# A hybrid encoder block on one core: its opening reordered on all engines

## The chip, the cores and the metric

The kernel runs on one core of a Trainium2 chip. The metric is the device time of one execution in microseconds (us). The engines are TensorE (PE in the profile, PEld for its weight loads), VectorE (DVE), ScalarE (ACT), GpSimd (POOL) and SyncE (SP, which issues DMAs). The granted TensorE clock has two levels, 1.2 and 2.4 GHz; 1.00 in a row is the upper one and 0.50 the lower.

## The reference

One block over 512 tokens of width 1024, in float32. x is RMS-normalised to h, h is projected by w_in, three branches run on the projections, and their gated outputs are merged, projected and added to x.

```
h = rms_norm(x, norm_g); proj = h @ w_in
A: mLSTM scan over q_a, k_a (after a causal conv), v_a, input and forget gates if_a
B: scores = sum_h relu(rot(qi_h) . rot(ki) / 8) * wi_h   # 8 index heads of 64
   per query the best 128 admissible keys, then attention of 8 heads on them
M: mem_h = rms_norm(mem, mem_norm_g); kv = mem_h @ w_mem_kv    # 256 memory tokens
   attention of 4 heads of 256 on the memory
x + (sum_j sigmoid(gate_j) * (y_j @ w_branch_j)) @ w_out
```

Rotary embeddings need the cosine and sine of position times inv_freq (angles).

## The kernel before

A float32 operand is split in two float32r parts: the high part is a rounding copy on ScalarE, the low part is the operand minus the high part, on VectorE. A product of two operands is three TensorE products: high by high, high by low, low by high.

**Panels.** The weights come in panels of up to 512 columns. A panel has two halves (kh = 0, 1) of four k tiles of 128 rows. For each half: SP loads it in w_raw (L324), ScalarE makes w_hi (`split_hi`, L751, 128x2048), VectorE makes w_lo (`split_lo`, L1069), and TensorE runs one block for each output tile: 12 products of 512 columns (4 k tiles by 3, `products`, L391). The buffer has one place for each half, so w_hi of the next panel waits until TensorE has used this one's half. A panel's blocks are numbered as slots through both halves (0 to 3 with two tiles). A hook is other TensorE work put ahead of the block of a slot; it waits for its inputs with the whole TensorE queue behind it.

**Order.** Each engine executes its own list in the order in which it is written; the engines meet at semaphores only. No planner is at work. The opening goes as follows.

1. x tiles 1, 2, 3, 0 (`FIRST_TILES`): ScalarE sums squares (L768), VectorE makes the variance, GpSimd the power -1/2 (L1570), VectorE scales the rows by it and by norm_g (L1092). TensorE turns each tile in two halves of four 128x128 transposes (L442), ScalarE writes the high parts hT_hi (L774) and VectorE the low parts hT_lo (L1100). mem's two tiles go the same way into memT_hi and memT_lo, but GpSimd scales them, in two passes each (L1581, L1582).
2. Index panel 1 (`IDX1`): the index queries of tokens 128 to 511 (three tiles), with the transposes of the later x tiles as hooks.
3. The angles: VectorE waits for inv_freq and positions (L1123 to L1134, twelve steps on 128x256 values), ScalarE takes the sines (L796, L797), VectorE copies them into tables for the index heads (L1141), GpSimd multiplies them with gains for branch B (L1590, eight products).
4. Index panel 2 (`IDX2`, the narrow panel): index key, head weights and mLSTM gates, 80 columns, with a panel turn of its own; its rows arrive by four DMAs (L348, L350).
5. Four memory panels 0 to 3 (`KV`) make the keys and values of the memory. Their hooks carry the index branch: `ki_transposes`, `gates_to_rows`, `idx_transposes` in panel 0, then eight `logit`s in each of panels 1 to 3, two a slot. A logit has six (or three) products on 64 rows; ScalarE applies relu (L829), VectorE adds it to the scores (L1220, L1222). logit(u) waits for the relu of logit u - 3. ScalarE's Exp and Ln for the mLSTM gates (L839, L840, a table load each) stand in panel 1 before the relus. The prefix scans over the gates (`gate_scans`, L1206 to L1211) stand on VectorE at the end of panel 1. The mean squares of the memory keys are a 128x2048 square on GpSimd (L1595) and a sum on VectorE (L1252) in panel 2.
6. The first cross-attention panel (`MS`) has `gates_to_columns` (L534) ahead of its first block, which waits for the gate scans (`gate_rows`) and for all 24 score sums, and `km_transposes` (L544) ahead of its fourth.

After that come the branches M, B and A and the merging, untouched by the change.

Of the kernel before, what the change touches and what calls it, by code (L numbers as in the profile page):

```python
# [23 lines left out]
FIRST_TILES = (1, 2, 3, 0)  # L24
A_HEADS, A_HD = 4, 256
# [61 lines left out]
IDX2 = _plan.take(1, 0, (1, 0, 0, 0))  # L87
# [37 lines left out]
def hybrid_block(nc, x, mem, positions, norm_g, mem_norm_g, w_in, conv_w, conv_b, mlstm_gate_b,  # L125
                 mlstm_norm_g, dsa_q_norm_g, dsa_k_norm_g, mem_q_norm_g, mem_k_norm_g,
                 w_mem_kv, w_branch, w_out, inv_freq, out):
    ctx = ExitStack()
    with ctx:
# [38 lines left out]
        idx2_raw = arena[:, 8 * D - 2 * KH * I_COLS:8 * D].rearrange("p (h k n) -> p h k n", h=2, k=KH)  # L168
        vec_rows = arena[0:92, 5 * D:5 * D + P]
        gain_rows = arena[:, 7 * D + P:7 * D + 3 * P]  # L170
        memT_hi = y_hi
        memT_lo = y_lo

        kiT = [y[:, 0:2, MEM:] for y in (y_hi, y_lo)]
        qiT = [[y[:, 2 * t:2 * t + 2, MEM:] for t in range(1, TT)] for y in (y_hi, y_lo)]
# [3 lines left out]
        ki_rot = yF[:, 3584:4096].rearrange("p (t n) -> p t n", t=TT)  # L181
# [9 lines left out]
        qi_b = arena[:, 8 * D:8 * D + 512]  # L191
        kiF = arena[0:I_COLS, 8 * D + 512:9 * D]

        km_raw = merged[:, 2048:4096]
        km_sq = arena[:, 4096:6144]
# [57 lines left out]
        w_hi_done, w_lo_done, w_used = sem("w_hi_done"), sem("w_lo_done"), sem("w_used")  # L253
        proj_done = [sem(f"proj_done{b}") for b in range(4)]
# [11 lines left out]
        idx_turned, idx_copied, ki_copied = sem("idx_turned"), sem("idx_copied"), sem("ki_copied")  # L266
        ki_turned, ki_rotated, q_split = sem("ki_turned"), sem("ki_rotated"), sem("q_split")
# [47 lines left out]
        def _(sp):  # L315
            def load(p, parts):

                for kh in range(2):

                    narrow = isinstance(p, int) and p == IDX2[0] + 1  # L320
                    sp.wait_ge(w_lo_done, IDX2[0] * 2 + (kh - 1) if narrow else p * 2 + (kh - 1))
                    at = 0
                    for w, c0, n in parts:
                        sp.dma_start(w_raw[:, kh, :, at:at + n], w_cols(w, kh * KH, c0, n)).then_inc(w_landed[kh], 16)  # L324
                        at += n
# [7 lines left out]
            sp.dma_start(w_raw[:, 0], w_cols(wi, 0, C_QI, 512)).then_inc(w_landed[0], 16)  # L333
            load_x(FIRST_TILES[2:])
            sp.dma_start(w_raw[:, 1], w_cols(wi, KH, C_QI, 512)).then_inc(w_landed[1], 16)
# [11 lines left out]
            for kh in range(2):  # L347
                sp.dma_start(idx2_raw[:, kh, :, 0:I_HD + I_HEADS], w_cols(wi, kh * KH, C_KI, I_HD + I_HEADS))\  # L348
                    .then_inc(idx2_landed, 16)
                sp.dma_start(idx2_raw[:, kh, :, I_HD + I_HEADS:], w_cols(wi, kh * KH, C_IF, 2 * A_HEADS))\  # L350
                    .then_inc(idx2_landed, 16)
# [32 lines left out]
        def _(pe):  # L384
            mm, turn = nc.tensor.matmul, nc.tensor.transpose

            def products(ps, lhs, rhs, k0, first, last):

                for k in range(KH):
                    for j, (a, b) in enumerate(((0, 0), (0, 1), (1, 0))):  # L390
# [43 lines left out]
            def x_transposes(i):  # L434

                pe.wait_ge(x_scaled, i + 1)
                for half in range(2):
                    n = 2 * i + half
                    if n >= 4:
                        pe.wait_ge(xT_lo, n - 3)  # L440
                    for k in range(4):
                        ins = turn(att[n % 4][:, k * P:(k + 1) * P],  # L442
                                   x_sc[:, i % 2, (half * 4 + k) * P:(half * 4 + k + 1) * P], ident[:, :])
                    ins.then_inc(x_turned, 1)
# [5 lines left out]

            pe.wait_ge(consts, 4)
            for i in range(2):
                x_transposes(i)

            panel(IDX1[0], [(t, 0, tokens(hT, t), w_as_rhs(512), 512, [(xT_lo, 2 * FIRST_TILES.index(t) + 2), None])
                            for t in range(1, TT)],
                  {1: [lambda: x_transposes(TT - 2)], 2: [lambda: x_transposes(TT - 1)], 4: [lambda: x_transposes(TT)],
                   5: [lambda: x_transposes(TT + 1), vector_transposes]})  # L460

            pe.wait_ge(xT_lo, 2 * TT)
            for kh in range(2):
                pe.wait_ge(w_lo_done, IDX2[0] * 2 + kh + 1)
                ins = products(banks[0][0:I_COLS, :], [lambda k, k0, w=w: w[:, kh, k, 0:I_COLS] for w in (w_hi, w_lo)],
                               all_tokens(hT)(kh), kh * KH, kh == 0, kh == 1)
                ins.then_inc(proj_done[0] if kh else w_used, 1)
# [10 lines left out]
            def gates_to_rows():  # L478
                pe.wait_ge(gates_copied, 1)
                pe.wait_ge(vec_copied, 1)  # L480
                pe.wait_ge(xT_lo, 2 * (TT + MT))
                for kind in range(2):
                    for t in range(TT):
                        ins = turn(att[kind][0:A_HEADS, t * P:(t + 1) * P],
# [3 lines left out]
            def idx_transposes():  # L488
                pe.wait_ge(qi_rotated, 3)
                pe.wait_ge(ki_rotated, 1)  # L490
                pe.wait_ge(gates_read, 1)
                for t in range(3):
                    for j in range(4):
                        ins = turn(att[t][:, j * P:(j + 1) * P], qi_rot[:, t, j * P:(j + 1) * P], ident[:, :])
# [1155 lines left out]
```

## Time and profile before

| | |
|---|---|
| device time, median of 3 runs | 1050.3 us (1049.99 to 1051.4) |
| span of the profiled execution (its own time: the page gives none beside the span) | 1049.9 us |
| TensorE busy | 1022.1 us, 97% |
| VectorE busy | 563.3 us, 54% |
| ScalarE busy | 403.7 us, 38% |
| GpSimd busy | 85.5 us, 8% |
| mean granted clock | 0.993 |

The span runs from the first to the last instruction of one execution. Busy time is the time with an instruction of that engine at work; a matmul's end is modelled, so consecutive ones overlap in the record. The time of a block is best read from the chain of waits, where a piece lasts until the next one begins.

### The profile page before, as it was taken

How to read it: one execution, taken by the hardware profiler on the slowest of the kernel's cores; microseconds unless marked ns; L12 is line 12 of the kernel's file. 1: busy time of each engine (PE TensorE's matmuls, PEld its weight loads, DVE VectorE, ACT ScalarE, POOL GpSimd, SP SyncE). 2: the span in 40 equal slices, each digit the busy share in tenths (PEclk: the TensorE clock that was granted, in tenths of full speed). 3: DMA queues.
4: the chain of work that ended last, by engine and by line, in shares of the span. 5: the costliest groups of instructions: out<-in, count | busy, mean ns of one | idle time of the engine just before them, and what ended most of it. 6: DMA issues, size and time to landing. Idle time of an engine off the chain costs nothing.

```text
span 1049.9 us, 13242 instructions
## 1 busy us (share of the span) xinstructions
PE 1022.1 (97%) x4965; PEld 856.2 (82%) x4965; DVE 563.3 (54%) x919; ACT 403.7 (38%) x567; POOL 85.5 (8%) x66
## 2 busy tenths in 40 slices
PE   5799999999999999999999999999999999999998
PEld 4577787778888888898898798787987888788887
DVE  4968686666854544544545645327353243532352
ACT  5264453433534434434435453444334422412230
POOL 1501010110110110110110000000000000000000
PEclk9899999999999999999999999999999999999999
DMA  9144421222233223223232222231312424234331
GB/s 300 41 138 132 126 86 41 70 62 61 61 91 90 75 75 90 75 75 90 73 98 81 66 95 61 61 120 53 107 61 61 120 81 120 81 86 144 130 101 60
DMA packets 110664, 95.42 MB, mean 91 GB/s; under 512 B 6344, under 2 KB 100900, under 8 KB 110628
## 3 DMA queue, kind: packets, MB, share of 16 engines
q1 hardware_dynamic: 109812, 94.37, 29.9%
q10 hardware_dynamic: 816, 0.56, 0.2%
q8 instruction: 24, 0.39, 0.2%
q14 instruction: 12, 0.10, 0.0%
HBM read 92.82 MB, written 2.10 MB: 90 GB/s over the span
## 4 chain that ended last, share of the span: by engine, by line
PE 91%; DVE 6%; ACT 2%; issue 1%; DMA 0%; POOL 0%; DVEq 0%; ACTq 0%; POOLq 0%
PE proj L391 78%; PE att L686 2%; PE att L618 2%; PE att L673 2%; PE att L633 2%; PE att L582 1%; DVE w_lo L1069 1%; PE att L562 1%; ACT w_hi L751 1%; PE att L625 1%; PE att L512 1%; PE att L608 1%; DMA yF<-x_in 0%; DVE score L1266 0%; DVE small L1264 0%
## 5 line engine op out<-in xcount | busy, mean ns | idle before, releaser
L1069 DVE TENSOR_TENSOR w_lo<-w_raw,w_hi 128x2048 fp32r<-128x2048 f32 (+2 forms) x94 | 198.4, 2111 | 271.7 <-ACT w_hi L751 269.9
L391 PE MATMUL proj<-hT_hi,w_hi 128*128 128x512 f32 (+1 forms) x648 | 257.2, 397 | 0.0
L391 PE MATMUL proj<-hT_hi,w_lo 128*128 128x512 f32 (+1 forms) x648 | 253.0, 390 | 0.0
L391 PE MATMUL proj<-hT_lo,w_hi 128*128 128x512 f32 (+1 forms) x648 | 252.7, 390 | 0.0
L751 ACT ACTIVATE w_hi<-w_raw 128x2048 fp32r<-128x2048 f32 (+2 forms) x94 | 159.3, 1695 | 211.4 <-PE proj L391 211.2
L391 PEld LDWEIGHTS proj<-hT_hi,w_hi 128*128 128x128 f32 (+1 forms) x648 | 121.6, 188 | 28.6 <-issue 4.0
L391 PEld LDWEIGHTS proj<-hT_hi,w_lo 128*128 128x128 f32 (+1 forms) x648 | 121.4, 187 | 25.9
L391 PEld LDWEIGHTS proj<-hT_lo,w_hi 128*128 128x128 f32 (+1 forms) x648 | 121.5, 188 | 25.7 <-issue 1.1
L391 PE MATMUL proj<-w_hi,hT_hi 128*128 128x384 f32 (+2 forms) x408 | 138.6, 340 | 2.8 <-DVE w_lo L1069 2.8
L391 PE MATMUL proj<-w_hi,hT_lo 128*128 128x384 f32 (+2 forms) x408 | 133.4, 327 | 0.0
L391 PE MATMUL proj<-w_lo,hT_hi 128*128 128x384 f32 (+2 forms) x408 | 133.4, 327 | 0.0
L391 PEld LDWEIGHTS proj<-w_hi,hT_hi 128*128 128x128 f32 x408 | 78.4, 192 | 6.8 <-DVE w_lo L1069 3.2
L391 PEld LDWEIGHTS proj<-w_lo,hT_hi 128*128 128x128 f32 x408 | 78.5, 192 | 3.5 <-issue 1.9
L391 PEld LDWEIGHTS proj<-w_hi,hT_lo 128*128 128x128 f32 x408 | 78.3, 192 | 1.4
L391 PE MATMUL proj<-y_hi,w_hi 128*128 128x512 f32 x192 | 76.0, 396 | 2.1 <-DVE y_lo L1075 1.2
L391 PE MATMUL proj<-y_hi,w_lo 128*128 128x512 f32 x192 | 74.9, 390 | 0.0
L391 PE MATMUL proj<-y_lo,w_hi 128*128 128x512 f32 x192 | 74.9, 390 | 0.0
L391 PE MATMUL proj<-w_hi,y_hi 128*128 128x512 f32 x128 | 52.3, 408 | 1.6 <-DVE w_lo L1069 1.6
L391 PE MATMUL proj<-w_lo,y_hi 128*128 128x512 f32 x128 | 50.7, 396 | 0.0
L391 PE MATMUL proj<-w_hi,y_lo 128*128 128x512 f32 x128 | 50.7, 396 | 0.0
L391 PEld LDWEIGHTS proj<-y_hi,w_hi 128*128 128x128 f32 x192 | 36.1, 188 | 10.0 <-issue 2.9
L391 PEld LDWEIGHTS proj<-y_hi,w_lo 128*128 128x128 f32 x192 | 36.1, 188 | 7.6
(229 smaller groups left out, 1153.0 us busy)
## 6 DMA issues: line engine op xcount, KB each, us to landing
w_raw<-w_in_in SPq DMA_DIRECT2D x72, 512.0 KB, 4.0
w_raw<-w_in_in SPq DMA_DIRECT2D x80, 256.0 KB, 3.2
w_raw<-w_mem_kv_in SPq DMA_DIRECT2D x8, 1024.0 KB, 5.1
w_raw<-w_branch_in SPq DMA_DIRECT2D x16, 512.0 KB, 5.0
yF<-x_in SPq DMA_DIRECT2D x8, 512.0 KB, 7.3
w_raw<-w_branch_in SPq DMA_DIRECT2D x16, 256.0 KB, 3.5
w_raw<-w_out_in SPq DMA_DIRECT2D x4, 1024.0 KB, 5.0
w_raw<-w_in_in SPq DMA_DIRECT2D x2, 1024.0 KB, 11.2
```

What stands on the lines that cost most here:

```text
L391: ins = mm(ps, lhs[a](k, k0), rhs[b](k, k0), start=(first and k == 0 and j == 0), stop=(last and k == KH - 1 and j == 2))
L512: ins = mm(att[u % 4][:, half * MEM:half * MEM + w], q[a], kiT[b][lo:lo + I_HD, half, 0:w], start=(j == 0), stop=(j == 2))
L562: ins = mm(att[1 + t // 2][:, (t % 2) * MEM:(t % 2 + 1) * MEM], m_qT[:, e, t * P:(t + 1) * P], kh_[:, bass.ds(h * 512 + e * MEM, MEM)], st ...
L582: ins = mm(att[1 + e][:, :], m_vh[:, m, e * P:(e + 1) * P], m_pT[:, m, :], start=(m == 0), stop=(m == MT - 1))
L608: ins = turn(att[c][:, t * P:(t + 1) * P], b_rc[:, (2 * t + c) * P:(2 * t + c + 1) * P], ident[:, :])
L618: mm(att[(t + 2) % 4][:, 0:(t + 1) * P], b_qT[:, t * P:(t + 1) * P], b_kT[:, 0:(t + 1) * P], start=True, stop=True).then_inc(b_scores, 1)
L625: ins = turn(att[(t + 2) % 4][:, s * P:(s + 1) * P], score[:, off(t) + s * P:off(t) + (s + 1) * P], ident[:, :])
L633: ins = mm(att[2][:, s * P:S], b_raw[:, s, 2 * P:3 * P], b_pT[:, s, s * P:S], start=(s == 0), stop=(s == TT - 1))
L673: ins = mm(att[bank][:, c:c + n], a_kT[:, e, s * P:(s + 1) * P], a_qT[:, e, s * P:S], start=(e == 0), stop=(e == 1))
L686: ins = mm(att[t][:, 0:A_HD + 1], a_at[:, c:c + P], a_v[:, s, :], start=(s == 0), stop=(s == t))
L751: A_(w_hi[:, kh, :, 0:n], raw[:, kh, :, 0:n], ACT.Copy).then_inc(w_hi_done, 1)
L1069: V.tensor_tensor(w_lo[:, kh, :, 0:n], raw[:, kh, :, 0:n], w_hi[:, kh, :, 0:n].bitcast(F32), ALU.subtract).then_inc(w_lo_done, 1)
```

## The change

The opening is put in another order on every engine, and some of its work changes its form:

- ScalarE no longer loads norm_g; it issues positions (as a contiguous array of 4 columns) and inv_freq first. SP issues: x tiles 1 and 2, norm_g, both halves of the first weights, x tiles 3 and 0, the narrow panel's rows in one DMA, mem, the small ones.
- VectorE starts with the angles up to the reduction by multiples of 2 pi, before the first variance; the last four steps follow after the fourth low part of x.
- The first half of the first weights is split for each k tile (four high and four low parts of 128x512), and TensorE's first block waits for each.
- x tiles are turned by halves in the order `TURNS`; block order is 1/0, 2/0, 1/1, 2/1, 3/0, 3/1 (tile/half).
- mem rows are scaled on VectorE in one pass.
- The narrow panel has buffers of its own and is no panel turn any more; the memory panels move up by one.
- Query and key of the index branch are split in high and low parts before they are transposed; 64 rows of high and 64 of low parts stand under each other. A logit is two products on 128 rows over the whole width. This takes 24 + 8 transposes instead of 12 + 4, and eight copies on ScalarE (`idx_copy`); low parts by VectorE are `q_lows` and `k_lows`.
- The logits are spread by `LOGIT_SLOTS`: none in slot 0 of panel 1, then 2, 2, 2; 3, 2, 3, 2 in panel 2; 3, 2, 2, 1 in panel 3.
- Squares of the memory keys come from ScalarE, two of 256 columns with each of the four evacuations. GpSimd's table products wait for the sixteenth score sum.
- Exp and Ln move from panel 1 to panel 2, the gate scans from panel 1 to the end of panel 3.

```diff
+TURNS = ((0, 0), (1, 0), (0, 1), (1, 1), (2, 0), (2, 1), (3, 0), (3, 1), (4, 0), (4, 1), (5, 0), (5, 1))
+LOGIT_SLOTS = ((), (0, 0, 2, 4, 6), (6, 9, 11, 14, 16), (16, 19, 21, 23, 24))
-IDX2 = _plan.take(1, 0, (1, 0, 0, 0))
+IDX2 = _plan.take(0, 0, (1, 0, 0, 0))
 # SP
             load_x(FIRST_TILES[:2])
+            sp.dma_start(g_row, norm_g.partition_broadcast(P)).then_inc(g_landed, 16)
+            for kh in range(2):
+                sp.dma_start(w_raw[:, kh], w_cols(wi, kh * KH, C_QI, 512)).then_inc(w_landed[kh], 16)
             load_x(FIRST_TILES[2:])
+            sp.dma_start(idx2_raw, w_idx2).then_inc(idx2_landed, 16)
 # TensorE
+            for n in range(4):
+                x_transposes(n)
+            idx_block(1, 0, 1, [(w_first_lo, 1), (w_first_lo, 2), (w_first_lo, 3), (w_lo_done, 1)])
+            idx_block(2, 0, 2)
+            pe.wait_ge(w_lo_done, 2)
+            idx_block(1, 1, 3).then_inc(proj_done[1], 1)
+            x_transposes(4)
+            x_transposes(5)
+            idx_block(2, 1, 4).then_inc(proj_done[2], 1)
+            x_transposes(6)
+            x_transposes(7)
+            idx_block(3, 0, 5).then_inc(w_used, 1)
+            idx_block(3, 1, 6).then_inc(proj_done[3], 1)
+            x_transposes(8)
+            x_transposes(9)
...
+            def q_transposes(f):
+                bank = (0, 1, 2, 0, 2, 0)[f]
+                t = f // 2
+                pe.wait_ge(q_low, t + 1)
+                if f == 0:
+                    pe.wait_ge(vec_copied, 1)
+                    pe.wait_ge(xT_lo, 2 * (TT + MT))
...
+                q = idxT[2 * (t - 1) + h // 4][:, h % 4 * P:(h % 4 + 1) * P]
+                n = (t + 1) * P
+                mm(att[u % 4][:, 0:n], q, idxT[6][:, 0:n], start=True, stop=False)
+                mm(att[u % 4][:, 0:n], q, idxT[7][:, 0:n], start=False, stop=True).then_inc(logits, 1)
 # hooks of memory panel i
+                    return {1: [ki_transposes, lambda: q_transposes(0), lambda: q_transposes(1)],
+                            2: [lambda: q_transposes(2), lambda: q_transposes(3)], 3: [gates_to_rows]}
+                marks = LOGIT_SLOTS[i]
+                hooks = {s: [lambda u=u: logit(u) for u in range(marks[s], marks[s + 1])] for s in range(4)}
+                if i == 1:
+                    hooks[0] = [lambda: q_transposes(4), lambda: q_transposes(5), k_transposes]
 # ScalarE
             square(0)
             square(1)
+            act.wait_ge(w_landed[0], 16)
+            for k in range(KH):
+                A_(w_hi[:, 0, k, :], w_raw[:, 0, k, :], ACT.Copy).then_inc(w_first_hi if k < KH - 1 else w_hi_done, 1)
+                if k < 2:
+                    x_high(k)
             x_high(2)
+            split_hi(0, 1, 1, 512)
             x_high(3)
             square(2)
             square(3)
...
+            x_high(8)
+            x_high(9)
+            split_hi(1, 0, KV[1] + 1, 512)
+            x_high(10)
+            split_hi(1, 1, KV[1] + 1, 512, (3, 1))
+            x_high(11)
             act.wait_ge(proj_done[0], IDX2[2][0] + 1)
             A_(kiF, banks[0][0:I_COLS, :], ACT.Copy).then_inc(bank_empty[0], 1)
+            for t in range(3):
+                q_highs(t)
 # ScalarE, memory panel i
-                if i == 1:
+                if i == 2:
                     act.wait_ge(gate_abs, 1)
                     steps.then(A_(rows[:, 3], rows[:, 2], ACT.Exp, scale=-1.0))
                     A_(rows[:, 3], rows[:, 3], ACT.Ln, bias=1.0).then_inc(gate_ln, 1)
...
+                        for e in range(2):
+                            g = m * M_HEADS + 2 * i + e
+                            A_(km_junk, banks[b][:, e * M_HD:(e + 1) * M_HD], ACT.Square, accum_out=kss[:, g:g + 1])\
+                                .then_inc(km_squared, 1)
+                            act.wait_ge(km_squared, i * 4 + m * 2 + e + 1)
 # VectorE
+            rotate_queries(1)
+            x_low(8)
+            x_low(9)
+            split_lo(1, 0, 512)
+            rotate_queries(2)
+            x_low(10)
+            split_lo(1, 1, 512)
+            x_low(11)
...
+            rotate_queries(3)
+            for t in range(3):
+                q_lows(t)
...
-                if i == 1:
+                if i == 2:
+                    dve.wait_ge(km_squared, 8)
+                    V.tensor_scalar(kss, kss, 1.0 / M_HD, EPS, ALU.mult, ALU.add).then_inc(km_var, 1)
+                if i == 3:
                     gate_scans()
-                if i == 2:
-                    dve.wait_ge(km_squared, 1)
-                    then(V.tensor_reduce(kss, km_sq.rearrange("p (g n) -> p g n", n=M_HD), AX, ALU.add))
 # GpSimd
             pool.wait_ge(small_landed, 16 * 4)
+            pool.wait_ge(summed, 16)
```

## Rows read from the trace of the kernel before

**Rows 1.** The page: busy time of the engines, and engines' shares of the chain.
```profile
PE 1022.1 (97%) x4965; PEld 856.2 (82%) x4965; DVE 563.3 (54%) x919; ACT 403.7 (38%) x567; POOL 85.5 (8%) x66
...
PE 91%; DVE 6%; ACT 2%; issue 1%; DMA 0%; POOL 0%; DVEq 0%; ACTq 0%; POOLq 0%
```

**Rows 2.** Waits of TensorE: us in total, times, longest us.
```profile
PE att L442 <- DVE arena L1092: 9.4, 1, 9.4
PE proj L391 <- DVE w_lo L1069: 4.5, 2, 2.8
PE att L442 <- DVE hT_lo L1100: 3.4, 1, 3.4
PE att L512 <- DVE w_lo L1069: 2.2, 1, 2.2
PE att L449 <- DVE y_lo L1100: 1.8, 1, 1.8
...
PE att L442 <- POOL arena L1582: 0.9, 1, 0.9
```

**Rows 3.** The chain of waits in order of time: start us, us, what.
```profile
16.19 5.49 PE proj L391 x12
...
33.02 0.43 DVE arena L1130
...
33.94 2.01 DVE arena L1130
...
44.26 7.94 PE proj L391 x24
...
66.32 1.31 PE att L494 x12
...
96.75 4.53 PE proj L391 x12
...
105.42 1.25 PE att L512 x12
106.67 2.94 PE proj L391 x12
...
122.80 8.41 PE proj L391 x36
```

**Rows 4.** One stretch: us, busy of PE, PEld, DVE, ACT, POOL, PEclk, DMA, GB/s.
```profile
40.00:50.00 10.00, 8.07 (x25) 6.26 (x26) 8.45 (x18) 3.17 (x7) 5.54 (x8) 0.54 0.01 2
```

**Rows 5.** Timeline of ScalarE: start us, us, line, operation [idle before].
```profile
71.37 1.91 ACT L751 ACTIVATE w_hi<-w_raw 128x2048 fp32r<-128x2048 f32 x1
73.29 1.28 ACT L839 ACT_TABLE_LOAD   x1
74.58 0.63 ACT L839 ACTIVATE merged<-merged 4x512 f32<-4x512 f32 x1
```

**Rows 6.** Timeline of VectorE, five rows between 8 and 92 us.
```profile
8.02 1.28 DVE L1092 SCALAR_TENSOR_TENSOR arena<-yF,small,arena 128x1024 f32<-128x1024 f32 x1 [0.74 <-POOL small L1570]
...
30.57 2.41 DVE L1128 TENSOR_SCALAR arena<-arena 128x256 f32<-128x256 f32 x1
...
58.43 2.29 DVE L1069 TENSOR_TENSOR w_lo<-w_raw,w_hi 128x2048 fp32r<-128x2048 f32 x1
...
86.56 4.00 DVE L1208 TENSOR_TENSOR_SCAN merged<-merged 4x512 f32<-4x512 f32 x1
...
91.31 1.21 DVE L1210 TENSOR_TENSOR_SCAN sig<-merged 4x512 f32<-4x512 f32 x1
```

**Rows 7.** Timeline of GpSimd.
```profile
7.42 0.56 POOL L1570 TENSOR_TENSOR small<-small,minus_half 128x1 f32<-128x1 f32 x1 [4.52 <-DVE small L1084]
...
30.47 2.37 POOL L1582 TENSOR_TENSOR arena<-arena 128x1024 f32<-128x1024 f32 x1
...
40.25 5.54 POOL L1590 TENSOR_TENSOR tabs<-arena 128x256 f32<-128x256 f32 x8 [2.10 <-ACT arena L797]
...
85.88 3.60 POOL L1595 TENSOR_TENSOR arena<-merged 128x2048 f32<-128x2048 f32 x1 [40.09 <-ACT merged L856]
```

**Rows 8.** DMA issues: tensors, engine, count, KB, us from issue to landing.
```profile
arena<-norm_g_in ACTq DMA_DIRECT2D x1, 512.0 KB, 5.4
...
arena<-inv_freq_in ACTq DMA_DIRECT2D x1, 32.0 KB, 10.0
...
small<-positions_in ACTq DMA_DIRECT2D x1, 2.0 KB, 8.7
```

More of the change, by code:

```diff
@@ L385, in _, with products @@
             mm, turn = nc.tensor.matmul, nc.tensor.transpose
-            def products(ps, lhs, rhs, k0, first, last):
+            def products(ps, lhs, rhs, k0, first, last, before_k=None):
                 for k in range(KH):
+                    if before_k is not None:
+                        pe.wait_ge(*before_k[k])
                     for j, (a, b) in enumerate(((0, 0), (0, 1), (1, 0))):
@@ L431, in y_split, with x_transposes @@
                 return [(ys_lo, (times - 1) * KT + (kh + 1) * KH) for kh in range(2)]
-            def x_transposes(i):
+            def x_transposes(n):
+                i, half = TURNS[n]
                 pe.wait_ge(x_scaled, i + 1)
[L437 to L444, printed above, removed]
+                if n >= 4:
+                    pe.wait_ge(xT_lo, n - 3)
+                for k in range(4):
+                    ins = turn(att[n % 4][:, k * P:(k + 1) * P],
+                               x_sc[:, i % 2, (half * 4 + k) * P:(half * 4 + k + 1) * P], ident[:, :])
+                ins.then_inc(x_turned, 1)
             def vector_transposes():
@@ L785, in _ @@
             square(3)
-            x_high(4)
-            x_high(5)
-            split_hi(0, 1, 1, 512)
-            for i in range(TT, TT + MT):
-                square(i)
-            x_high(6)
-            x_high(7)
             act.wait_ge(ang_ready, 1)
@@ L842, in _ @@
                     gate_copies()
+                    idx_copy(0)
+                    idx_copy(1)
+                    k_highs()
+                elif i == 1:
+                    for f in range(4, 8):
+                        idx_copy(f)
+                    relus(marks[0], marks[2])
                 else:
[L844 removed]
+                    relus(marks[0], marks[2])
                 split_hi(p + 1, 0, KV[1] + i + 2 if i < 3 else MS[1] + 2, 512)
                 if i:
[L847 removed]
+                    relus(marks[2], marks[4])
                 else:
[L849 removed]
+                    idx_copy(2)
+                    idx_copy(3)
                 for m in range(MT):
@@ L1101, in x_low @@
                                 hi[at].bitcast(F32), ALU.subtract).then_inc(xT_lo, 1)
+            dve.wait_ge(ang_landed, 16 * 2)
+            then(V.tensor_copy(pos_f, pos_i))
+            ang3 = ang.rearrange("p (t n) -> p t n", t=TT)
+            then(V.tensor_tensor(ang3, invf.unsqueeze(1).to_broadcast([P, TT, 64]),
+                                 pos_f.unsqueeze(2).to_broadcast([P, TT, 64]), ALU.mult))
+            then(V.tensor_scalar(turns, ang, INV_2PI, ROUNDER, ALU.mult, ALU.add))
+            then(V.tensor_scalar(turns, turns, -ROUNDER, None, ALU.add))
+            for part in (TWO_PI_HI, TWO_PI_MID, TWO_PI_LO):
+                then(V.scalar_tensor_tensor(ang, turns, -part, ang, ALU.mult, ALU.add))
             x_variance(0)
@@ L1211, in gate_scans, with sums @@
                 V.tensor_tensor(rows[:, 1], rows[:, 3], maxrow, ALU.add).then_inc(gate_rows, 1)
-            def sums(i, part):
-                for u in range(8 * i + 4 * part, 8 * i + 4 * part + 4):
-                    t, h = u // 8 + 1, u % 8
+            def sums(lo, hi):
+                for u in range(lo, hi):
+                    t, h = u // I_HEADS + 1, u % I_HEADS
                     acc = score[:, off(t):off(t + 1)]
```

300 lines of the change are left out of this document (140 added, 160 removed).

## The prediction

> **What bounds the kernel now.** I read the page's busy shares and chain first: TensorE is busy for 97% of the span and carries 91% of the chain [rows 1]. A change pays only through TensorE: less work, fewer waits, or less time at the low clock. Its waits come next: 9.4, 4.5 (in two places), 3.4, 2.2, 1.8 and 0.9 us, together 22.2 us, all before 96 us [rows 2]. After 131 us it is dense, so what the opening gains or loses there arrives at the end unchanged. My sum is therefore made for one moment: TensorE's end of the third block of the first cross-attention panel, 122.80 + 8.41 = 131.2 us before [rows 3].
>
> The same chain shows the clock. A block of 12 products takes 2.94 us at full rate with its hand-over (2.81 alone); the first took 5.49 us, the one behind the 2.2 us wait 4.53, and 24 products at 44 us took 7.94, their first half at the low pace [rows 3], with a granted clock of 0.54 from 40 to 50 us [rows 4], mostly the 1.2 GHz level. So a wait of 2 us or more brings another 1.6 to 2.6 us of slow products behind it.
>
> **The change part by part.** I walked each engine's queue in the new order with row durations: ScalarE 1.91 us for a 128x2048 high part, 0.60 for 128x512, 1.28 for a table load [rows 5]; VectorE 2.29 for a 128x2048 low part, about 0.68 for 128x512, 1.28 for a row scaling [rows 6]; 0.56 for a power on GpSimd [rows 7].
>
> *Angles ahead of x.* VectorE now waits first of all for inv_freq and positions. Before, inv_freq landed 10.0 us after issue (at 11.7), positions 8.7 us after, both queued behind the gain row, which took 5.4 us for 128 pieces beside x [rows 8]. Now they head ScalarE's queue at 0.7 and 1.2 us, and positions come as 128 pieces, not 512. Bounds: x's first tile (4.7 us, without the gain row beside it) less a little, say 4, and the old 11.7. Nearest is the gain row: two loads of 128 small pieces beside x, so I take 6.0 us. Seven steps of 0.2 to 0.43 us (as the first two of line 1130, GpSimd being free [rows 3]) with hand-overs make 2.75: 8.75. Variance, power and scaling follow: the scaling starts at 9.6, not 8.02 [rows 6]; the gain row, third in SP's queue, lands by 7.4, hidden. TensorE starts at 10.9 instead of 9.45 and waits 1.0 for the second tile: 2.4 lost.
>
> *First weights per k tile, tiles by halves.* The low parts come at 14.0, 14.6, 15.9 and 16.5, the 16 transposes end at 15.85, products start there and not at 16.19; the 2.8 us wait goes. Nothing is late next: the blocks run on to 35.3, and the second half's split (18.0 to 20.3) is needed at 22.3.
>
> *GpSimd out of the way.* Line 1128 took 2.41 us beside line 1582's 2.37 on GpSimd; the first two steps of line 1130 took 0.43 each, the third, beside the next GpSimd row, 2.01 [rows 3, 6, 7]. Four steps were stretched by some 7.5 us in all, and TensorE's waits of 0.9, 3.4 and 1.8 us hang on this and on the mem rows. They go. On VectorE the mem rows are two scalings, 1.28 each, with a 0.7 us wait for each power; they end at 34.5 and 36.5, hidden behind products (wanted at 35.3 and 39.0). If that cover failed, each us late is a us. The narrow panel ends at 42.3 (55.0 before); its load is one transfer instead of four.
>
> *What is late then.* TensorE reaches the memory panels at 42.9, not 56.6, 13.7 us ahead, and meets VectorE and ScalarE, which are not: 1.2 us for kiF's copy and 0.65 for the last x_low (47.5); then the query transposes in slot 1 need q_low, and VectorE does a low part (44.6 to 46.9), the third rotation (to 49.8) and q_lows first: 2.7 us, to 50.5. With the slow block behind it (1.6), 6.2 of the 13.7 are given back; the bound is zero if VectorE is 4 us earlier.
>
> *High and low parts paired.* 16 transposes more, at 1.31/12 = 0.11 each: +1.75 us. The logits were 8 pairs at 1.25 [rows 3] and 4 (256 columns a product, not 384 and 512) at about 0.8: 13.2 us. They become two products over the whole width: 2 x 8 x (256+384+512) = 18,432 columns at 2.73/6144 us, 8.2, and 0.7 for switching: 8.9, so -4.3. Products on 128 rows aren't in the trace for this shape of logit; the blocks' products, 128 rows too, cost the same per column, and I keep 0 to -5.4 as bounds. The eight copies before logit 0 stand behind two evacuations now grown by two squares each (0.5 us apiece: 256 columns and a 0.2 us accumulator read; between 0.4 and 0.6) and a high part: logit 0 waits 1.2 us.
>
> *Exp and Ln.* Their table loads and passes are 2 x 1.28 + 2 x 0.63 = 3.8 us [rows 5] and stand before the relus. Before, they lay in panel 1, where logits 0 to 3 need no relu, and ended as slot 2 came. Now they lie in panel 2: logit 10, in slot 1, needs the relu of logit 6, queued behind the evacuation (1.6), the high part (1.9) and the 3.8. ScalarE is ready 8.2 us after the panel began (79.0), TensorE after 4.1: a wait of 4.1 us, and 2.3 of slow products.
>
> *Gate scans.* They leave panel 1, where they made a low part late (the 2.2 us wait and 1.8 at low clock: gone), and stand after the last score sums of panel 3. The next hook on TensorE, the gate transposes, needs them; before they were 29 us old by then. Line 1208's 4.00 us ended 1.1 us after GpSimd's 3.60 us square; alone it is like line 1210, 1.2. So the six steps are 0.69+0.50+1.2+0.69+1.2+0.68 and hand-overs, 5.2 us [rows 6, 7] (8 if the 4.00 stays). The last sum ends 0.2 us before TensorE is through with the panel (115.5), by which TensorE waits for 5.1 us, and 2.4 to 2.9 us of low clock follow. The next low part and km_normed come within 5 us of it, in cover (9 us of blocks).
>
> **The sum.** Before minus after, at TensorE: memory panels start 56.6 and 44.05; panel 1 70.8 and 63.2; panel 2 84.9 and 79.0; panel 3 101.3 and 100.4; gate transposes 122.2 and 120.6 (reached at 115.5); third block done 131.2 and 132.5. So 12.5 us of lead come down to -1.3. Span 1049.9 + 1.3 = 1051.2; the page has no other time of that execution, the median run of 1050.3 is 0.4 above the span, and the forecast is 1051.6.
>
> **Rules of the Trainium skill weighed.** Only sentences here rest on them. DMA: Bandwidth & Descriptors, section "Queues, rings and completion order", says an engine of the DMA drains a whole packet of some 9 to 17 descriptors from one ring before it turns to the next; the eight pieces per engine of each small load would then go in one turn, and the angles land with x's first tile. By that rule the result is rival A; the 10.0 us of inv_freq speak against it. SBUF — State Buffer, section "Who interferes with whom", has VectorE instructions with two SBUF inputs contend with GpSimd; by that rule the result is rival D, and the 2.01 us of line 1130's third step agree.
>
> **The rivals.** A: the angles land at 4. The walk gives 2.1 us less: 1049.5. For it: small loads at the head of a queue; against: the old landings.
> B, the slower one: the angles land late. Place: VectorE's first wait, everything of VectorE behind it. Each us after 6.0 moves the scaling and the walk's end by 1.0; it decides from 6.9 on, and at 10 costs 4.1: 1055.7. For it: 8.7 and 10.0 us before; against: those stood behind 512 KB and 512 pieces.
> C: one of the two late waits doesn't stand, since VectorE or ScalarE gets there 4 to 5 us sooner than walked (a shorter evacuation, earlier sums). 4.1 + 2.3 or 5.1 + 2.6, less what the other takes over: about -6, 1045.6. Against it: both follow from the order of the queues.
> D: the eight GpSimd table products (5.5 us in all, 0.7 each [rows 7]) now start at the sixteenth sum, beside five score sums. Up to 0.69 on each, of which 2 us are slack: +0.9 on the walk, with a second load of a table for the mem squares (1.28, of which 0.7 shows) +1.6: 1053.2.
>
> **How the numbers follow.** Chances: forecast 0.45, A 0.15, B 0.15, C 0.15, D 0.10. What a measurement can tell from no change is 0.2%, 2.1 us. The forecast's own range is 1050 to 1053.5, from how long each slow stretch lasts (1.3 us either way) and the squares; so 0.33 of it is "same" and 0.12 slower. A gives 0.10 same, 0.05 faster; B and D slower but for a trace; C faster. Faster 0.20, same 0.43, slower 0.37. The range 1046.3 to 1055.5 takes in most of B and C.
>
> **What would show it.** The first scaling near 9.6 us and first transposes near 10.9; angle steps of 0.3 to 0.43 us, none of 2; no wait of TensorE between 16 and 42 us; waits of about 2.7, 4.1 and 5.1 us before the query transposes, in the second slot of panel 2 and before the gate transposes, each followed by a slow block; scans of 1.2 us each; logit pairs of 0.5 to 1.0 us. It is wrong if TensorE reaches the first memory panel after 46 us, or if the gate transposes don't wait. Below 1047 I have overrated the late waits, above 1055 underrated the first.

## The result: 0.36% slower, and the profile after

The changed kernel takes 1054.5 us (median of 6 runs, 1051.6 to 1056.3), the kernel before 1050.2 (6 runs, 1050.0 to 1051.4). The ratio is 1.0036, 95% interval 1.0021 to 1.0050: slower by 4.3 us, where 1.3 was forecast. The profiled execution is the slowest of the six, 1056.3 us with a span of 1054.3. The six runs lie 5 us apart: the three longest had a mean granted clock of 0.990, the three shortest 0.992 to 0.993.

The page, busy time by engine and shares of the chain, against [rows 1]:

```profile
PE 1019.5 (97%) x4909; PEld 857.7 (81%) x4909; DVE 553.5 (52%) x919; ACT 412.4 (39%) x594; POOL 77.3 (7%) x61
PE 89%; DVE 6%; ACT 2%; issue 2%; DMA 1%; POOL 0%; ACTq 0%; DVEq 0%; POOLq 0%
```

TensorE is 2.6 us less busy than before, slow products included, and its share of the chain falls by 2 points: the loss is not more work. Its waits (us in total, times, longest) answer to [rows 2]:

```profile
PE att L444 <- DVE arena L1145: 13.4, 2, 12.5
PE att L560 <- DVE merged L1287: 6.1, 1, 6.1
PE att L535 <- ACT yF L864: 4.4, 1, 4.4
PE att L514 <- DVE arena L1234: 2.4, 1, 2.4
...
PE proj L394 <- ACT arena L841: 1.2, 1, 1.2
PE att L535 <- ACT y_lo L832: 0.9, 1, 0.9
...
PE att L489 <- DVE y_lo L1153: 0.8, 1, 0.8
```

These add up to 29.2 us, the six of [rows 2] to 22.2: 7.0 us more waiting less 2.6 us of busy time is the 4.4 us between the spans. The old 4.5 us (in two places), 3.4, 2.2, 1.8 and 0.9 are gone; the first wait grew from 9.4 to 13.4. In the place of the others stand three late ones: 6.1 us before the gate transposes (L560), 4.4 in the second slot of panel 2 (L535), 2.4 before the query transposes (L514). The chain of waits, in order of time (start, us, what):

```profile
1.18 6.31 DMA arena<-inv_freq_in
...
11.10 1.28 DVE arena L1145
14.47 2.82 PE att L444 x12
17.29 9.77 PE proj L394 x36
...
52.21 1.97 PE att L514 x8
54.17 4.62 PE proj L394 x12
...
90.80 5.06 PE proj L394 x12
118.40 0.69 DVE merged L1282
119.76 1.22 DVE merged L1284
...
123.75 0.98 PE att L560 x8
124.73 10.80 PE proj L394 x36
```

The third block ends at 124.73 + 10.80 = 135.5, where it was 131.2 before [rows 3]. That is 4.3 of the 4.4 us between the spans (1054.3 and 1049.9). A block behind each late wait is slow: 4.62 and 5.06 us instead of 2.75, and 10.80 for three blocks instead of 8.41. The stretches of 10 us round them (TensorE's granted clock is the third number from the end), against 0.54 at 40 to 50 us before [rows 4]:

```profile
40.00:50.00 10.00, 7.83 (x40) 5.47 (x38) 9.93 (x15) 4.94 (x7) 0.00 (x0) 1.00 0.34 110
50.00:60.00 10.00, 7.79 (x31) 6.67 (x32) 5.24 (x13) 3.71 (x8) 0.00 (x0) 0.66 0.30 101
90.00:100.00 10.00, 10.00 (x35) 8.37 (x36) 4.55 (x7) 4.15 (x7) 0.00 (x0) 0.72 0.26 97
120.00:130.00 10.00, 6.25 (x21) 5.16 (x22) 9.79 (x13) 1.57 (x3) 0.00 (x0) 0.66 0.34 105
```

So 1.2 GHz in part of three stretches, each entered out of a wait. How the lead over the kernel before was won and lost:

| TensorE reaches | before | predicted | after | lead predicted | lead found |
|---|---|---|---|---|---|
| memory panel 0 | 56.6 | 44.05 | 45.6 | 12.5 | 11.0 |
| panel 1 | 70.8 | 63.2 | 66.05 | 7.6 | 4.75 |
| panel 2 | 84.9 | 79.0 | 81.3 | 5.9 | 3.6 |
| panel 3 | 101.3 | 100.4 | 102.95 | 0.9 | -1.65 |
| gate transposes begin | 122.2 | 120.6 | 123.75 | 1.6 | -1.6 |
| third block done | 131.2 | 132.5 | 135.5 | -1.3 | -4.3 |

The DMA issues at the head of ScalarE's queue and the gain row (last number: us from issue to landing), against [rows 8]:

```profile
arena<-norm_g_in SPq DMA_DIRECT2D x1, 512.0 KB, 7.4
arena<-inv_freq_in ACTq DMA_DIRECT2D x1, 32.0 KB, 6.3
small<-pos_cols_in ACTq DMA_DIRECT2D x1, 2.0 KB, 3.8
```

And, from VectorE's and GpSimd's timelines, the angle steps of line 1164 and the score sums beside the table products (start, us, form, count):

```profile
8.83 1.34 DVE L1164 SCALAR_TENSOR_TENSOR arena<-arena 128x256 f32<-128x256 f32 x3
108.80 4.54 DVE L1298 SCALAR_TENSOR_TENSOR score<-yF,small,score 128x512 f32<-128x512 f32 x4
115.86 2.32 DVE L1298 SCALAR_TENSOR_TENSOR score<-yF,small,score 128x512 f32<-128x512 f32 x3
103.57 9.22 POOL L1648 TENSOR_TENSOR tabs<-arena 128x256 f32<-128x256 f32 x8 [66.50 <-DVE score L1298]
```

Three angle steps take 1.34 us with GpSimd free, 0.43 each. A sum takes 1.12 us while GpSimd works and 0.76 once it has stopped. The eight products take 9.2 us and not 5.5 [rows 7]: their median is 1.05 us, and one takes 2.82, as VectorE makes the low part of 105.59 to 107.88 beside it.

### The profile page after: what moved, and what is told of

It reads as the page before. It is cut to its first block, busy times and chain, and to the rows that moved or that the text cites. A ratio compares the mean times of both kernels' runs of the same rounds, so it can differ in the third digit from the quotient of the medians.

```text
span 1054.3 us, 13146 instructions
## 1 busy us (share of the span) xinstructions
PE 1019.5 (97%) x4909; PEld 857.7 (81%) x4909; DVE 553.5 (52%) x919; ACT 412.4 (39%) x594; POOL 77.3 (7%) x61
## 4 chain that ended last, share of the span: by engine, by line
PE 89%; DVE 6%; ACT 2%; issue 2%; DMA 1%; POOL 0%; ACTq 0%; DVEq 0%; POOLq 0%
PE proj L394 76%; PE att L712 2%; PE att L644 2%; PE att L699 2%; PE att L659 2%; PE att L608 1%; ACT w_hi L776 1%; DVE w_lo L1119 1%; PE att L588 1%; PE att L651 1%; DVE score L1298 1%; PE att L634 1%; DMA arena<-inv_freq_in 1%; DVE score L1335 0%; DVE small L1333 0%
## 5 line engine op out<-in xcount | busy, mean ns | idle before, releaser
L1119 DVE TENSOR_TENSOR w_lo<-w_raw,w_hi 128x2048 fp32r<-128x2048 f32 (+2 forms) x93 | 196.1, 2109 | 285.5 <-ACT w_hi L776 283.6
L394 PE MATMUL proj<-hT_hi,w_hi 128*128 128x512 f32 x640 | 254.8, 398 | 0.0
L394 PE MATMUL proj<-hT_hi,w_lo 128*128 128x512 f32 x640 | 250.4, 391 | 0.0
L394 PE MATMUL proj<-hT_lo,w_hi 128*128 128x512 f32 x640 | 250.3, 391 | 0.0
L394 PEld LDWEIGHTS proj<-hT_hi,w_hi 128*128 128x128 f32 x640 | 120.8, 189 | 28.3 <-issue 4.0
L394 PEld LDWEIGHTS proj<-hT_hi,w_lo 128*128 128x128 f32 x640 | 120.7, 189 | 25.6
L394 PEld LDWEIGHTS proj<-hT_lo,w_hi 128*128 128x128 f32 x640 | 120.8, 189 | 25.2 <-issue 1.0
```

The source lines that it names most:

```text
L394: ins = mm(ps, lhs[a](k, k0), rhs[b](k, k0), start=(first and k == 0 and j == 0), stop=(last and k == KH - 1 and j == 2))
L1119: V.tensor_tensor(w_lo[:, kh, :, 0:n], w_raw[:, kh, :, 0:n], w_hi[:, kh, :, 0:n].bitcast(F32), ALU.subtract).then_inc(w_lo_done, 1)
```

## The experiments

Ratios are against the kernel before on the same chip, where its median was 1050.3 to 1051.4. Each kernel ran 4 to 11 times.

**r1, the changed kernel again.** No edit.

> The changed kernel once more, unchanged. My theory: its times spread over 1051.5 to 1056.5 us because the slow-clock stretches behind its three late waits last a different time in each execution; the waits themselves (2.4, 4.4 and 6.1 us) come out within 0.3 us again, and the median is 1053 to 1055. Rival (the spread comes from the DMAs of the opening): the first scaling of x moves by more than 1 us between executions.

Measured: 1054.0 us (1051.5 to 1056.2), ratio 1.0034 (1.0022 to 1.0046). The loss is real, and so is the spread: the same waits of 6.1, 4.4 and 2.4 us in another execution, and the clock goes with the time (0.993 at 1051.5, 0.990 at 1056.2). The rival finds no support: the first scaling starts at 10.97 us, 0.13 before the other execution's. Of the 0.7 us between the two spans, 0.5 are shorter slow products (9.49, 4.48, 4.98 and 10.76 us for 9.77, 4.62, 5.06 and 10.80). Both profiled executions are long ones, 1055.7 and 1056.3; none near 1051.5 was profiled.

**r2, angles later.** They leave the head of VectorE's queue, and ScalarE's sines go behind the high parts 4 to 7 of x.

```
             x_low(4)
             x_low(5)
+            dve.wait_ge(ang_landed, 16 * 2)    # all eleven angle steps, moved here
             x_low(6)
             x_low(7)
...
 # ScalarE
+            for n in range(4, 8):
+                x_high(n)
             act.wait_ge(ang_ready, 1)
...
-            for n in range(4, 8):
-                x_high(n)
```

> The angles stand behind the sixth low part of x and no longer ahead of x. Theory: the first scaling starts when the gain row has landed, about 9.0 us instead of 11.1; the rest of the opening keeps its distance, less up to 1.5 us where the angles now delay the mem rows: 1 to 2 us faster than the changed kernel, about 1052.5. Rival (the first wait is the whole loss): 3.6 us faster, since the scaling could start at 7.5 as x allows. Rival (hidden): no difference, because all time of the opening before the memory panels is absorbed by their waits.

Measured: 1053.7 us (1052.4 to 1054.8), ratio 1.0029 (1.0019 to 1.0040): 0.4 to 0.9 us better than the changed kernel, within what can be told apart. The transposes start 1.9 us earlier (the chain has the second group at 12.53, not 14.47), the query transposes 1.3 us earlier (50.90, not 52.21), and the late waits stay at 6.1, 4.4 and 2.4 us. But 1.1 of those 1.3 us are the first three blocks, 8.67 us here and 9.77 there; in r4, whose opening is the changed kernel's, they took 8.47 us, and the query transposes began at 51.04. The lead is lost in a third wait on a scaling, 1.1 us before the transposes of mem, and the chain leads from there to ScalarE: high parts of x, the sines with their table load (L816), squares of mem, then VectorE's scaling:

```profile
PE att L444 <- DVE arena L1145: 12.6, 3, 10.6
```

```profile
29.23 1.14 ACT L816
...
31.88 1.04 ACT arena L791 x2
...
33.77 0.46 DVE arena L1145
```

Taking the late landing away in this manner is thus worth a small part of the loss. The scaling starts at 9.17, now behind the gain row, so r7 and r10 also put that row first in ScalarE's queue.

**r3, gate scans early.**

```
-                if i == 3:
-                    gate_scans()
+                if i == 2:              # behind the first sums of panel 2
+                    gate_scans()
                 split_lo(p + 1, 0, 512)
```

> The gate scans stand behind the first sums of memory panel 2, where VectorE was idle for 5.2 us, instead of the end of panel 3. Theory: the 6.1 us wait before the gate transposes goes and the slow products behind it (10.8 us for three blocks instead of 8.4, and 0.4 on the transposes) too: 8 to 9 us faster than the changed kernel, about 1046. Rival (VectorE is the bound of panel 3 through the sums beside GpSimd): only the 5.2 us of the scans, about 1049.5, with a wait left at the same place.

Measured: 1045.0 us (1044.5 to 1048.1), ratio 0.9954 (0.9942 to 0.9966): 9 us less than r1, and faster than before. The 6.1 us wait for the last scan has become a short one for the last sum:

```profile
PE att L560 <- DVE score L1298: 1.3, 1, 1.3
```

and behind it the chain has no slow block (three blocks in 8.39 us, not 10.80):

```profile
51.47 1.09 PE att L514 x8
52.56 2.75 PE proj L394 x12
...
114.79 0.63 PE att L560 x8
115.42 8.39 PE proj L394 x36
```

The first two of these lines are a surprise: the 2.4 us wait stands in this kernel too, and its block took 2.75 us here, 4.62 in the profiled execution of the changed kernel.

**r4, Exp and Ln behind the relus of logits 6 to 10.**

```
                 else:
                     relus(marks[0], marks[2])
+                if i == 2:                       # moved from ahead of the relus
+                    act.wait_ge(gate_abs, 1)
+                    ... Exp, Ln
```

> Exp and Ln with their table loads stand behind the relus 6 to 10 of panel 2, where ScalarE was idle for 3.9 us, instead of ahead of them. Theory: logit 10 waits 0.5 us and not 4.4, and the block behind it takes 2.8 us and not 5.1: 6 us faster than the changed kernel, about 1048.5, since the last sums and the scans behind them move with the logits. Rival (the gain is given back at the gate transposes): their wait grows from 6.1 us and the time falls by under 2 us.

Measured: 1051.4 us (1050.7 to 1055.6), ratio 1.0015 (1.0005 to 1.0024): 2.6 us less than r1, not 6. The waits for ScalarE are two now, 0.6 us and 2.8, since the next relus stand behind Exp and Ln instead; and the wait at the gates grew, for TensorE is there 5.7 us sooner than in the changed kernel's profile (111.9, not 117.6), the end of the scans only 4.4 (119.3, not 123.7):

```profile
PE att L560 <- DVE merged L1287: 7.5, 1, 7.5
PE att L535 <- ACT yF L864: 3.3, 2, 2.8
```

**r5, r3 with GpSimd's table products not waiting for the sixteenth sum.**

```
-            pool.wait_ge(summed, 16)
```

> The gate scans in panel 2 as in r3_scans_early, and GpSimd's eight table products no longer wait for the sixteenth score sum, so they run from about 26 us, beside the low parts of the opening. Theory (the pair of VectorE and GpSimd holds sums of two SBUF operands up): sums 16 to 20 take 0.76 us each again and not 1.1, the 1.3 us wait left before the gate transposes in r3_scans_early goes: 1 to 2 us faster than r3_scans_early, about 1043.5. Rival: the tables now stretch steps of the opening by as much and the time is that of r3_scans_early, 1045, or above.

Measured: 1045.7 us (1045.4 to 1047.2), ratio 0.9958 (0.9944 to 0.9972): r3's time. The sums take 0.76 us again and the 1.3 us at the gates went, but a wait in the opening (L489) grew from 0.8 to 1.8 us, for the products (9.1 us) now ran beside VectorE's work there. The contention was moved, not removed.

**r6, low parts of query tiles 0 and 1 ahead of the third rotation.**

```
+            q_lows(0)
+            q_lows(1)
             rotate_queries(3)
-            for t in range(3):
-                q_lows(t)
+            q_lows(2)
```

> On the changed kernel the first two q_lows stand ahead of the third rotation. Theory: the 2.4 us wait before the query transposes falls to about 0.2 us and the slow products behind it (1.1 us on the transposes, 1.8 on the block) go in most executions: 2 to 4.5 us faster than the changed kernel's 1054.3. Rival (given back): the later waits for Exp and Ln and for the scans grow by as much, no difference.

Measured: 1049.1 us (1048.5 to 1051.0), ratio 0.9991 (0.9982 to 1.0000), about 5 us less than the changed kernel. The 2.4 us wait is 0.4, the block behind it is quick, and the 6.1 us at the gates are untouched. Chain of waits:

```profile
49.22 1.09 PE att L514 x8
50.31 2.75 PE proj L394 x12
...
116.67 0.98 PE att L560 x8
117.65 10.03 PE proj L394 x36
```

**r7, all moves at once** (r2 with the gain row first in ScalarE's queue, r3, r4, r5, r6).

> Six moves at once on the changed kernel: angles behind the sixth low part, gain row back at the head of ScalarE's queue, gate scans in panel 2, Exp and Ln behind relus 6 to 10, table products from 26 us, q_lows ahead of the third rotation. Theory: no wait over 1.5 us is left between the first product and the cross-attention panels and the clock stays up after 20 us: waits of 2.4, 4.4 and 6.1 us and 5 to 7 us of slow products gone, 14 to 16 us faster than the changed kernel, about 1039.5. Rival: each move uncovers the next engine and the whole is worth less than scans early alone plus 3 us: 1042 or above.

Measured: 1044.2 us (1043.4 to 1044.6), ratio 0.9935 (0.9921 to 0.9949). The rival held. The first scaling started at 8.01 us and the transposes 3.1 us ahead of the changed kernel's, but new waits ate it:

```profile
PE att L534 <- ACT yF L864: 3.7, 3, 2.8
PE att L488 <- DVE y_lo L1153: 2.2, 1, 2.2
PE att L534 <- DVE w_lo L1119: 2.0, 1, 2.0
```

Ln ended at 90.35, the scans behind it filled VectorE from 90.46 to 95.7, and the low part and the sums after them were late. Moves that each help alone met in one queue.

**r8, the kernel before with mem's rows scaled on VectorE**, all else as it was.

```
-                V.scalar_tensor_tensor(x_sc[:, i % 2, :], x_in[:, FIRST_TILES[i]], xrs[:, i:i + 1], g_row,
-                                       ALU.mult, ALU.mult).then_inc(x_scaled, 1)
...
+                src, g = (x_in[:, FIRST_TILES[i]], g_row) if i < TT else (mem_in[:, i - TT], memg_row)
+                V.scalar_tensor_tensor(x_sc[:, i % 2, :], src, xrs[:, i:i + 1], g, ALU.mult, ALU.mult)\
+                    .then_inc(x_scaled, 1)
...
 # GpSimd
-                    steps.then(G.tensor_tensor(row, mem_in[:, i - TT], xrs[:, i:i + 1].to_broadcast([P, D]), ALU.mult))
-                    G.tensor_tensor(row, row, memg_row, ALU.mult).then_inc(x_scaled, 1)
```

> The kernel before with one part of the change alone: the mem rows are scaled by VectorE in one pass each ahead of the angles. Theory (GpSimd's passes stretched the angle steps): lines of the angle steps take 0.3 to 0.43 us each, none 1.9 or 2.4; the 0.9 us wait goes, the 3.4 us one falls to about 1.7, and the narrow panel starts 3 us earlier: 3 to 5 us faster than before, about 1046.5. Rival (the steps are slow by themselves after the clamp of the kernel's first us): steps stay and 2.6 us of scaling come on top, 2 us slower.

Measured: 1046.6 us (1046.5 to 1048.3), ratio 0.9964 (0.9950 to 0.9978): 3.7 us less than before by this one part. The angle steps are short again; chain of waits:

```profile
32.40 0.44 DVE arena L1135
...
39.44 7.19 PE proj L391 x24
```

The narrow panel's blocks start at 39.4 and not at 44.3 [rows 3]. The 0.9 us wait is gone and the 3.4 us one is 1.1. GpSimd's square of the memory keys stays in this kernel, and the scan beside it still takes 4.00 us, as in [rows 6].

**r9, two moves: r3 and r6.**

> Two edits on the changed kernel: the gate scans behind the first sums of panel 2 (r3) and the low parts of query tiles 0 and 1 ahead of the third rotation (r6); Exp and Ln stay ahead of the relus of panel 2. Theory (late waits are independent, each with its slow stretch, as long as nothing stands behind Exp and Ln on VectorE): the two gains add, 1054.3 - 9.3 - 5.2 = 1039.8 us (1038 to 1041.5), waits of 2.4 and 6.1 us gone, the 4.4 us one stays. Rival (the lead of the one is eaten by the other: TensorE, 4 us earlier in panel 2, waits longer for the relus and the scans): 1042.5 to 1044.

Measured: 1042.9 us (1042.2 to 1044.2), ratio 0.9925 (0.9911 to 0.9938), 3.0 us below r3 by the ratios. Of both waits 0.4 and 1.7 us are left and the 4.4 us one stands, as the theory had it, but the time is in the rival's range (before was at 1051.4 on this chip, which is 1 us of it). The mechanism is not the rival's, no wait has grown by more than 0.4 us; in r3's profiled execution the 2.4 us wait had no slow block behind it to be saved.

**r10, r9 with the opening of r7.** The angles as in r2, and the gain row taken from SP's queue:

```
-            sp.dma_start(g_row, norm_g.partition_broadcast(P)).then_inc(g_landed, 16)
...
+            act.dma_start(g_row, norm_g.partition_broadcast(P)).then_inc(g_landed, 16)
             act.dma_start(pos_i, pos_cols)
```

> r9 and beside it the opening of r7: the angles behind the sixth low part of x and the gain row at the head of ScalarE's DMA queue. Theory A (the late waits take up most of what the opening wins, since VectorE then does the angle steps later): first transposes 3 us earlier, but no more than 1 us less than r9. Theory B (a lead at the start arrives at the end once the waits are gone): 2 to 3 us less than r9.

Measured: 1041.7 us (1040.8 to 1042.2), ratio 0.9909 (0.9894 to 0.9924). The transposes start 3.0 us earlier than in r9 (second group 11.31, not 14.28), the query transposes 1.0 us (48.87, not 49.91), and the gates 1.0 us; the medians differ by 1.3, and the intervals of the ratios overlap. That is theory A, a little above its 1 us: two thirds of a lead at the start go by the time of the query transposes. The first three blocks took the same in both (9.81 and 9.70 us). What takes the lead is r2's third wait again, 1.1 us before mem's transposes, and 0.4 us more at L488. On the chain stands ScalarE's queue, sines ahead of mem's squares; VectorE's angle steps end at 30.3 us, 0.25 before the first sine, so they are nearly as late. No run moved one of the two alone.

```profile
11.31 2.82 PE att L443 x12
...
48.87 1.09 PE att L513 x8
```

**r11, r9 with the table products behind the last sum.**

```
-            pool.wait_ge(summed, 16)
+            pool.wait_ge(summed, 24)
```

> r9, but GpSimd's eight table products wait for the last score sum (24), not the sixteenth. It tests whether the products and the sums stretch each other: theory: the four sums from the twentieth on take 0.76 us each beside no GpSimd work (1.1 before), GpSimd's products 0.7 to 0.8 us instead of 1.15 wherever VectorE has no sums; the time comes out 0 to 1 us below r9. Rival: the sums were slow for another reason (their operands are 512 columns in any case), they stay at 1.1 us, and the time is r9's.

Measured: 1045.7 us (1044.2 to 1046.0), ratio 0.9943 (0.9930 to 0.9957), 2.8 us more than r9. The mechanism is as the theory says: the sums take 0.76 us each and the products 0.74 (median of the eight), but for one of 2.79 us from 114.29 on, beside VectorE's low part of 114.04 to 116.48, itself 2.44 us and not 2.29. Chain of waits:

```profile
109.80 0.76 DVE score L1299
...
112.20 6.96 POOL tabs L1649 x7
119.16 1.62 POOL small L1652
```

and the 1.7 us at the gates vanish. But the power for the memory keys stands behind the products on GpSimd; it started at 119.16 and took 1.6 us, and TensorE waited for the keys:

```profile
PE att L570 <- DVE merged L1381: 2.7, 1, 2.7
```

**r12, the best version that the runs point to:** r10 with Exp and Ln between panel 1's first relus and its high part, and the products behind the last sum and behind that power.

> r10 with two more moves. Exp and Ln go to panel 1, between its first relus and its high part: there ScalarE was idle for 2.4 us in r10 and the gates lie ready 5 us before; the high part comes 1.4 us later. GpSimd's eight table products wait for the last sum and stand behind the power for the memory keys, so that neither the sums (1.1 us each in r10) nor the keys wait for them. Theory (each late wait was one of order alone): the 4.4 us wait of panel 2 and its slow block (4.96 us in r11, 2.2 above a quick one) go, up to 1 us comes back as a wait at the start of panel 2: 5 to 6 us less than r10, 1035.5 to 1037 us. Rival (VectorE and ScalarE are the bound in panels 1 to 3: the lead ends as waits for sums, relus or low parts): 1038.5 to 1041.

Measured: 1040.7 us, four runs within 0.1 us, ratio 0.9906 (0.9889 to 0.9922): 10 us faster than before, 14 faster than the change. Of r10 it is 1.0 us better by the medians, and by ratio not told apart from it; the rival held. The waits of panels 2 and 3:

```profile
PE att L534 <- ACT yF L864: 2.3, 2, 1.9
PE att L559 <- DVE score L1299: 0.8, 1, 0.8
```

The 4.4 us are 1.9, and yet w_lo of panel 3 starts at 91.71 us, in r10 at 91.88. Panel 1's high part came 1.8 us late (70.83, not 69.03), so the evacuations, panel 2's high part (79.33, not 77.63) and its low part did too. The first sums of panel 2 stand behind that low part and start at 83.54, in r10 at 83.71: they gained nothing. From there to 94.5 us the chain is VectorE's alone (sums, scans, a low part), and after that VectorE's and ScalarE's in turn (relus, evacuations, high parts), but for 0.75 us; TensorE only waits for them in one place or another. A slow block stands in this execution too, 4.11 us from 48.93 on; the waits ahead of it are those of r10 (1.2 and 0.4 us), where the block took 2.77.

## Why the prediction was half right

The forecast of a loss and its places held: three late waits predicted at 2.7, 4.1 and 5.1 us are there at 2.4, 4.4 and 6.1, each with a slow block. But the walk said 1.3 us and 4.3 came. Its own range ended at 1053.5 and the median is 1054.5, which only the width given for rival B takes in: that the stated range holds is in part luck. "Slower" had 0.37 and "same", within 2.1 us, 0.43, so the likelier of the two did not come. By its steps:

1. **Angles ahead of x: right place, undersized.** inv_freq landed 6.3 us after issue at 1.2, 7.5 and not 6.0. The steps took 2.7 us as said, and everything behind is 1.5 us late: scaling 11.1 (9.6), transposes 12.5 (10.9), products 17.3 (15.85), memory panels 45.6 (44.05). This is rival B's mechanism at 1.5 us. In the profiled execution the 1.5 us stand in the table as far as panel 0; in r4's, with the same start (products 17.2), panel 0 begins at 44.4, since its first blocks were quicker, so the slow products there weigh nearly as much as the landing. What an earlier start brings in the end is less: with the angles moved behind x, 1.9 us at the transposes brought 0.4 to 0.9 us and 3.0 brought 1.0 to 1.3 (r2, r10), none of it clear of the intervals, and 1.1 us of the lead goes into a wait for mem's scaling. By the Trainium skill (DMA: Bandwidth & Descriptors, "Queues, rings and completion order") a DMA engine drains a whole packet from one ring before it turns to the next; that had led to rival A, a landing with x's first tile. x's first tile was there at 4.4 us. Positions, with as many pieces of 16 bytes, landed 3.8 us after issue, at 4.5, as the rule would have it; inv_freq, right behind them, landed at 7.5 and did not. The gain row landed 7.4 us after its issue, at about 9.0, where the prediction had it landed "by 7.4"; it hid behind the angles all the same (the scaling waited for its power), and came out in r2.
2. **First weights per k tile: right.** The 2.8 us wait is gone, and from 17.3 to 42 us TensorE doesn't wait at all, as was said. (The 0.8 us of L489 come at 49.3, and were walked at 0.65.) The first three blocks took 9.77 us, 1.4 above three at 8.39.
3. **GpSimd out of the way: right.** Steps of 0.43 us, scans of 1.2 and not 4.0, and r8 alone brings 3.7 us to the kernel before.
4. **What is late then: right in place, half the size behind it.** 2.4 us (2.7), but the slow block cost (1.97 - 0.87) + (4.62 - 2.75) = 3.0 us, not 1.6. r6 shows it as a matter of order: two instructions moved, 5 us gained.
5. **Paired logits: right.** Two products of 384 columns take 0.35 us (L535 and L536 in the chains of r4), of 512 0.46. No run undid the pairing, so its worth of 4.3 less 1.75 us stays an estimate. Logit 0 waited 0.9 us and not 1.2.
6. **Exp and Ln ahead of the relus: right** (4.4 us for 4.1, slow block 2.3). What it is worth to take away was wrong in my later expectation for r4: what stands behind it in the queue gets its 3.8 us.
7. **Gate scans at the end of panel 3: right in place, 1 us short.** From 118.40 to 123.66 they take 5.3 us (5.2 predicted). TensorE was through with its panel at 117.6, and the last sum ended 0.6 us after that, not 0.2 before. The chain shows why: sums beside the products took 1.12 us, the relus wait for the sums and the next high part for the relus. That is rival D, with chance 0.10 and priced at 0.9 us; r11 removes it from r9, and 1.7 us at the gates go. The Trainium skill (SBUF — State Buffer, "Who interferes with whom") says that a VectorE instruction with two SBUF inputs contends with a GpSimd instruction that reads SBUF; the trace agrees: 1.12 against 0.76 us on VectorE, a median of 1.05 against 0.74 on GpSimd. r3 is the main proof of this step: 9 us, twice what the whole change lost.

So what failed is a sum of sizes, not a mechanism, as read in the profiled execution: 1.5 us of landing, 1.4 us more of slow products behind the first late wait, and 1.0 us at the gates, less 0.9 of small gains in panels 1 to 3, are the 3.0 us between 132.5 and 135.5. The cases had been laid out as alternatives, B or D, with the forecast's own waits; here B at 1.5 us and D came together with all of them. C did not happen. The median lies 4.3 us above before's, as the spans do (4.4); my 0.4 us between median and span was not that execution's own: runs of the kernel before with a span of 1049.9 took 1051.7 in the later sets, 1.8 above the span. It does no harm, since it falls out of the difference.

Left open: whether the 5 us between runs of one kernel is only the length of the slow stretches. The runs say that time and granted clock go together; what makes a stretch longer or absent in one execution they do not show. Open too are the pairing's own worth and which of the two queues, ScalarE's or VectorE's, holds the opening of r10 back.

## What to carry to other kernels

A reordering that wins time at the head of a pipeline pays only until the next engine that was not sped up with it: walk every queue to the end of the region, and give work that moved "out of the way" (scans, table loads, products) a place where its engine is idle and its result is due much later, since behind a wait of TensorE there may be as much again in slow products. Try each move alone and then together; here moves worth 9 and 5 us alone made 12 together (r9), and six together, two of them in each other's way, 10 (r7). A count in a semaphore wait of another engine (sixteenth or last sum) is a place in time too, and everything queued behind it moves with it.

## What the hardware showed that was not expected

- The slow block behind the same 2.4 us wait cost 3.0 us in the changed kernel's profiled execution, 1.6 in r2's, 1.8 in r4's and 0.2 in r3's (1.09 + 2.75 us against 0.87 + 2.75). A wait doesn't bring a fixed price. Nor does a slow block need a wait of 2 us: at the same place, behind waits of 1.2 and 0.4 us, it took 4.11 us in r12 and 2.77 in r10. Runs of r1 and r4 spread over 4.6 and 4.8 us, but those of r2, with the same three waits as r1, over 2.4; the four of r12 over 0.1.
- Two small loads of 128 pieces each, one behind the other on one queue, landed 3.8 and 6.3 us after issue beside x; behind a 512 KB row of the same queue they took 6.5 and 8.2 (DMA rows of r10), and the row itself 5.4.
- A GpSimd product of 0.74 us took 2.79 beside VectorE's 128x2048 low part (r11): it hardly moved until that was through, while the low part lost 0.15 us. In the kernel before it was the other way round: a scan of 1.2 us took 4.00 beside GpSimd's square of 3.60, which had started first [rows 6, 7]. Beside the sums both lost, a product 0.31 us and a sum 0.36.
